# Recurrence: the next pair's key panel inside the state walk, mixing read from the banks, the output in its own buffer beside the new keys, the gate one pair later

## The chip, the cores and the metric

One core of a Trainium2 chip. The metric is the device time of one launch, in microseconds (us). Engines: TensorE (PE; its weight loads are PEld), VectorE (DVE), ScalarE (ACT), GpSimd (POOL), SyncE (SP, which issues the weight DMAs).

## The reference, cut to what matters

Three layers over 512 tokens of width 1024: one with latent and sliding-window attention, one with forgetting attention, and one with an RWKV-7 recurrence beside a convolution. The change touches the recurrence of the third layer alone:

```
rkv = rkv + (shift(rkv) - rkv) * mu_rkv            # shift: the token before
w   = exp(-exp(-softplus(-(w0 + tanh(xw@w1)@w2)) - 0.5));  a = sigmoid(a0 + (xa@a1)@a2)
g   = sigmoid(xg @ g1) @ g2
kk  = k*k_k / max(norm(k*k_k), 1e-12);  k = k*(1 + (a-1)*k_a)
S_t = S_{t-1} diag(w_t) + (S_{t-1} (-kk_t)) (kk_t*a_t)^T + v_t k_t^T ;  o_t = S_t r_t     # per head, 64x64
o   = (o - mean) * rsqrt(var + 64e-5) * ln_g + ln_b            # per head
out = (o + sum(r*k*r_k) * v) * g
```

There are 16 heads of 64 columns.

## The kernel before, in words

Activations lie with features on partitions and the 512 tokens along the free axis. Every product with a weight matrix is done in panels: a panel is 128 output columns, its weights are 128x1024 floats in one of four slots. SP loads the panel into `raw` (L331), ACT casts it to a high part `wh` (`split`, L454), POOL forms the low part `wl` = raw - high (`low`, L1652), and PE multiplies three times per 128 rows (`three`, L1800 to L1802): 24 matmuls of 128x128 by 128x512. Panels are consumed strictly in the order in which `weight_stream` packs them. A slot is cast anew only when PE has counted `panel_done` for the panel that lay in it, and loaded anew when its low part is out.

The recurrence goes over eight pairs of heads (c = 0 to 7; 2 x 64 rows fill the partitions). Pair c takes four panels: a small one with the second factors of decay, rate and gate (`lora_part`), then k, r and v. `pair(c)` on PE issues, in this order: two eighths of the k panel, the mean of the last pair's output (`mean`, L2198), the gate's three matmuls into bank 4, three eighths of k, the variance (`by_token`, L2135), the rest of k, two eighths of r, `output_spread` (L2144, the inverse root spread over rows), more r, the key norm (`kk`, L2135), more r, `kspread` (L2144), the rest of r, all of v, and then `half(c)`. Banks 0 and 1 take turns for the dense tiles; ACT copies each out of its bank (`copy_tile`, L851) into zk, zr, zv, and DVE mixes each with its shifted self in two instructions (`shift`, L1448 and L1449).

`half(n)` is the chunked recurrence: 8 chunks of 64 tokens. Each product is a series of small fp32 matmuls of 64x64 (L2244), in groups g = 0 and 1: l, lr, kr, the bonus (L2193), ab, kv, then the levels that invert a triangular matrix, then tt, mp and n. l needs b (L1473), lr needs r (L1476), kr needs k (L1478). ab needs t1, made from l by DVE (`first_t`, L1527 and L1528, in `half`). The last part is the walk over the states, L2273 to L2286: for each of eight chunks, c (L2277), the output o (L2285, three terms, into the output bank), while DVE adds the next state (L1552). The next pair's decay and rate products are issued early in the levels (`decay_and_rate`).

After the walk ACT copies the output bank into zr (L922); zr holds the output of pair c-1 until DVE has centred it (L1489), scaled it (L1498), added the bonus (L1500) and gated it with the copied gate `gt` (L1502), ACT has taken its high part (L885) and DVE its low part (L1506). Only then may ACT copy the new r into zr. POOL does, within `half`, bd (L1754), kd (L1756), dg (L1757) and the masks of each level (L1765), and the low parts of the panels before and after.

The order on each engine is written out by hand; every engine works its own list in order and waits on counted semaphores.

Of the kernel before, what the change touches and what calls it, by code (L numbers as in the profile page):

```python
# [22 lines left out]
P = 128  # L23
T = 512
# [122 lines left out]
def build(nc, A, n_panels, b2_start):  # L147

    ctx = ExitStack()
    with ctx:  # L150
# [74 lines left out]
        with ExitStack() as part:  # L225


            z = [sb(f"z{n}", [P, T + 1], F32, part) for n in "rkv"]
            zr, zk, zv = (a[:, 1:T + 1] for a in z)
            gt = sb("gt", [P, T], F32, part)  # L230
# [6 lines left out]
            half_b = sb("half_b", [P, 16], F32, part)  # L237
            going = sb("going", [P, T], F32, part)
# [3 lines left out]
        cu, em, rn, kkn = s1, s1c, sd, rs  # L242
        la, lw = t2[:, 0, :], t2[:, 1, :]
# [117 lines left out]
        def groups(names):  # L361
# [4 lines left out]
            pair_act: ["decay", "square", "root", "gate"],  # L366
            pair_dve: ["sums", "mixed", "kmax", "kinverse", "prod"],
# [72 lines left out]
        def _(act):  # L440
# [383 lines left out]
            od0 = NC * 11  # L824

# [5 lines left out]
            def decay_tanh(c):  # L831
                act.wait_ge(mid_done, m0 + 2 * c + 1)
# [3 lines left out]
            def rate_tanh(c):  # L836
                act.wait_ge(mid_done, m0 + 2 * c + 2)
# [8 lines left out]
            def pair(c):  # L846

                def copy_tile(i, dst, p):
                    b = tile_bank(c, i)
                    act.wait_ge(panel_done, p0 + 4 * c + p)  # L850
                    nc.scalar.copy(dst, psum[:, b, :]).then_inc(bank_free[b], 1)  # L851
                if c == 0:
                    split(Idx(0, p0 + 3))
                else:
# [4 lines left out]
                st.did(pair_act, "square", nc.scalar.activation(sq[:, 0, :], zk, ACT.Square, scale=pcol("k_k", c)))  # L859
# [5 lines left out]
                act.wait_ge(panel_done, p0 + 4 * c + 1)  # L865
                st.did(pair_act, "gate", nc.scalar.copy(gt[:, :], psum[:, 4, :]))
                split(Idx(0, p0 + 4 * c + 5))
                act.wait_ge(opnd_dve, c + od0)
                copy_tile(3, zr, 3)
                copy_tile(4, zv, 4)  # L870
                half(c)

            def centred_square(c):

                st.wait(post_dve, c, "centred")
                st.did(post_act, "osquare", nc.scalar.activation(sq[:, 0, :], zr, ACT.Square))
# [5 lines left out]
            def high(c):  # L882

                st.wait(post_dve, c, "out")
                st.did(post_act, "high", nc.scalar.copy(bh[1][:, c, :], zr))  # L885

            def half(n):
# [31 lines left out]
                if not last:  # L919
                    split(Idx(0, p0 + 4 * n + 7))  # L920
                st.wait(half_pe, n, "o7")
                st.did(half_act, "o", nc.scalar.copy(zr, psum[:, O_BANK, :]))  # L922
# [9 lines left out]
            w.p += 4 * NC  # L932
            w.g += 6 * NC
            w.mid += 2 * NC
# [44 lines left out]
        def _(dve):  # L979
# [398 lines left out]
            nc.vector.memset(going[:, :].rearrange("p (a t) -> p a t", t=64)[:, :, 0:1], 0.0)  # L1378
            nc.vector.tensor_scalar(half_b[:, 0:8], par[:, PAR["w0"][0]:PAR["w0"][0] + 8], 0.5, None, ALU.mult)
# [41 lines left out]
            g0 = w.g  # L1421
# [22 lines left out]
            def pair(c):  # L1444

                def shift(i, dst):

                    link(V.tensor_tensor(sq[:, 0, :], z[i][:, 0:T], dst, ALU.subtract))  # L1448
                    return V.scalar_tensor_tensor(dst, sq[:, 0, :], pcol("mu_rkv", NC * i + c), dst, ALU.mult, ALU.add)  # L1449
# [15 lines left out]
                if c:  # L1465
                    output_low(c - 1)
# [17 lines left out]
                V.scalar_tensor_tensor(sq[:, 1, :], psum[:, b, :], 64.0, zv, ALU.mult, ALU.mult).then_inc(bank_free[b], 1)  # L1484
                half(c)

            def centre(c):
                st.wait(post_pe, c, "mean")
                st.did(post_dve, "centred", V.tensor_tensor(zr, zr, psum[:, 2, :], ALU.subtract))  # L1489
# [5 lines left out]
            def output(c):  # L1495

                st.wait(post_pe, c, "ospread")
                link(V.scalar_tensor_tensor(zr, zr, col("lnx_g", c), psum[:, 5, :], ALU.mult, ALU.mult))  # L1498
                tile_moved(c, 5)
                link(V.scalar_tensor_tensor(zr, zr, col("lnx_b", c), sq[:, 1, :], ALU.add, ALU.add))  # L1500
                st.wait(pair_act, c, "gate")
                st.did(post_dve, "out", V.tensor_tensor(zr, zr, gt[:, :], ALU.mult))  # L1502

            def output_low(c):
                st.wait(post_act, c, "high")
                V.tensor_tensor(bl[1][:, c, :], zr, bh[1][:, c, :].bitcast(F32), ALU.subtract).then_inc(opnd_dve, 1)  # L1506

            def half(n):
# [17 lines left out]
                def first_t(g):  # L1526
                    link(V.tensor_tensor(one(g, M_T), bank(f"l.{g}"), each(wm[:, 2, :]), ALU.mult))  # L1527
                    did(f"t1.{g}", V.tensor_tensor(one(g, M_T), one(g, M_T), each(eye[:, :]), ALU.add))  # L1528

# [3 lines left out]
                grouped("l", first_t)  # L1533
# [3 lines left out]
                grouped("ab", first_x)  # L1537
                beside = {8: decay_exponent, 16: decay_sums, 32: rates} if n < NC - 1 else {}
# [25 lines left out]
            output(NC - 1)  # L1564
            output_low(NC - 1)
            w.p += 4 * NC
# [76 lines left out]
        def _(pool):  # L1643
# [124 lines left out]
            def pair(c):  # L1768
# [6 lines left out]
                if c < NC - 1:  # L1775
                    low(Idx(0, p0 + 4 * c + 7))
# [4 lines left out]
            w.p += 4 * NC  # L1781
# [13 lines left out]
        def _(pe):  # L1795
# [327 lines left out]
            def decay_and_rate(c):  # L2123
                p = p0 + 4 * c
                pe.wait_ge(lo_ready, p + 1)
                lora_part(tile_bank(c, 0), p, slice(0, 64), 0, 0).then_inc(mid_done, 1)
                lora_part(tile_bank(c, 1), p, slice(64, 128), 0, 0).then_inc(mid_done, 1)

            def gate(c):
                lora_part(4, p0 + 4 * c, slice(0, 128), P, 1).then_inc(panel_done, 1)  # L2130
# [17 lines left out]
            def pair(c):  # L2148

                def dense_part(b, i, ks):  # L2150

                    p = p0 + 4 * c + i
                    s = p % SLOTS
                    pe.wait_ge(lo_ready, p + 1)
                    for k in ks:
                        if c == 0 and i == 1:
                            pe.wait_ge(opnd_pool, op0 + k + 1)
                        cols = slice(k * P, k * P + P)
                        last = three(psum[:, b, :], wh[:, s, cols], wl[:, s, cols], bh[0][:, k, :], bl[0][:, k, :],
                                     k == 0, k == NC - 1)  # L2160
                    return last
                b = tile_bank(c, 2)
                dense_part(b, 1, range(2))
                if c:
                    mean(c - 1)
                    gate(c)
                    dense_part(b, 1, range(2, 5))
                    variance(c - 1)
                    dense_part(b, 1, range(5, NC)).then_inc(panel_done, 1)
                else:  # L2170
                    dense_part(b, 1, range(2, NC - 1))
                    pe.wait_ge(lora_l, 2)
                    gate(c)
                    dense_part(b, 1, range(NC - 1, NC)).then_inc(panel_done, 1)
                b = tile_bank(c, 3)
                dense_part(b, 2, range(2))
                if c:
                    output_spread(c - 1)
                dense_part(b, 2, range(2, 4))
                st.wait(pair_act, c, "square")  # L2180
                st.did(pair_pe, "kk", by_token(6, sq[:, 0, :]))
                dense_part(b, 2, range(4, 6))
                st.wait(pair_dve, c, "kinverse")
                st.did(pair_pe, "kspread", spread(7, r8[:, 2, :]))
                dense_part(b, 2, range(6, NC)).then_inc(panel_done, 1)
                b = tile_bank(c, 4)
                dense_part(b, 3, range(NC)).then_inc(panel_done, 1)
# [7 lines left out]
            def mean(c):  # L2195
                st.wait(half_act, c, "o")
                st.wait(half_dve, c, "s8")
                st.did(post_pe, "mean", nc.tensor.matmul(psum[:, 2, :], o64[:, :], zr, start=True, stop=True))  # L2198

            def variance(c):  # L2200
                st.wait(post_act, c, "osquare")
                st.did(post_pe, "var", by_token(3, sq[:, 0, :]))
# [5 lines left out]
            def half(n):  # L2208
# [7 lines left out]
                def product(name, *outs, needs=()):  # L2216


                    for g in range(2):
# [3 lines left out]
                        if i == 2:  # L2223
# [257 lines left out]
```

## Time and profile before

| | us |
|---|---|
| median of 3 runs | 2743.78 (2743.17 to 2747.65) |
| profiled execution, its own time | 2744.07 |
| its span | 2742.2 |
| PE busy | 2553.0 (93%) |
| DVE busy | 1395.3 (51%) |
| POOL busy | 1147.4 (42%) |
| ACT busy | 910.6 (33%) |

The recurrence runs from about 1506 us to 2019 us of the span. Pairs repeat every 64.02 us: the copy of the output bank (L922) starts at 1822.29 and again at 1886.31. A row of the timeline gives start, duration, engine, line, operation, output and inputs, and in brackets the idle time before it with what ended it. Ends of matmuls are modelled, so the distance from start to start is what counts on PE.

### The profile page before, as it was taken

To read this page: it belongs to the slowest core of one execution; us is meant where nothing else is said; L and a number is where in the kernel's file an instruction comes from. 1 tells how busy PE (TensorE), PEld (TensorE's weight loads), DVE (VectorE), ACT (ScalarE), POOL (GpSimd) and SP (SyncE) were. 2 spreads that over 40 slices of the span, in tenths; PEclk is the share of its full clock that TensorE was granted. 3 is DMA by queue.
4 is the path that set the end of the run, shared out by engine and by line. 5 is a ranking of instruction groups with operands and counts; after the bars stand their busy time and mean duration, and the time that the engine had idled before them with its cause. 6 is when DMAs were issued, how large, how long until landed. Compare 5 with 4: busy or idle time off the path is not lost.

```text
span 2742.2 us, 46926 instructions
## 1 busy us (share of the span) xinstructions
PE 2553.0 (93%) x18466; PEld 2077.3 (76%) x18466; DVE 1395.3 (51%) x1997; ACT 910.6 (33%) x1444; POOL 1147.4 (42%) x657
## 2 busy tenths in 40 slices
PE   6798899999899998999996999999999988999998
PEld 4575688887787877888875888887887766788886
DVE  3624873345513258454277566666659963321122
ACT  3233422223523334222254333333333334332231
POOL 3433544444444435444454333333333325444442
PEclk8999999999999999999998999999999999999999
DMA  5310223232221112323322111111112222233331
GB/s 152 80 54 16 85 92 100 92 100 85 77 93 35 58 62 85 99 92 94 98 71 73 41 33 41 41 33 33 33 57 87 89 62 83 87 99 98 94 100 54
DMA packets 56465, 202.67 MB, mean 74 GB/s; under 512 B 6768, under 2 KB 7448, under 8 KB 56304
## 3 DMA queue, kind: packets, MB, share of 16 engines
q1 hardware_dynamic: 54144, 195.84, 22.5%
q0 software_dynamic: 1328, 3.68, 0.8%
q8 instruction: 124, 2.03, 0.3%
q10 hardware_dynamic: 832, 0.82, 0.1%
q14 instruction: 37, 0.30, 0.0%
HBM read 196.64 MB, written 3.67 MB: 73 GB/s over the span
## 4 chain that ended last, share of the span: by engine, by line
PE 78%; DVE 11%; issue 4%; ACT 4%; POOL 2%; DMA 0%; DVEq 0%; SPq 0%; ACTq 0%; POOLq 0%
PE banks L1800 21%; PE banks L1801 21%; PE banks L1802 21%; PE banks L2244 8%; ACT sb_pa L635 1%; PE banks L2285 1%; DVE banks L1592 1%; PE banks L2018 1%; DVE sb_zr L1502 1%; POOL sb_pa L1678 1%; PE banks L1980 1%; DVE sb_x L1078 1%; PE banks L2144 1%; PE banks L1933 1%; PE banks L2001 1%
## 5 line engine op out<-in xcount | busy, mean ns | idle before, releaser
L1652 POOL TENSOR_TENSOR sb_wl<-sb_raw,sb_wh 128x1024 fp32r<-128x1024 f32 x365 | 897.3, 2460 | 1235.9 <-ACT sb_wh L454 1235.7
L1800 PE MATMUL banks<-sb_bh,sb_wh 128*128 128x512 f32 x2656 | 1061.8, 400 | 93.9 <-POOL sb_bl L1664 28.0
L1801 PE MATMUL banks<-sb_bl,sb_wh 128*128 128x512 f32 x2656 | 1047.1, 394 | 0.0
L1802 PE MATMUL banks<-sb_bh,sb_wl 128*128 128x512 f32 x2656 | 1045.9, 394 | 0.0
L1800 PEld LDWEIGHTS banks<-sb_bh,sb_wh 128*128 128x128 f32 x2656 | 505.4, 190 | 227.4 <-issue 53.9
L1802 PEld LDWEIGHTS banks<-sb_bh,sb_wl 128*128 128x128 f32 x2656 | 505.1, 190 | 110.5
L1801 PEld LDWEIGHTS banks<-sb_bl,sb_wh 128*128 128x128 f32 x2656 | 505.8, 190 | 107.4 <-issue 2.2
L454 ACT CAST sb_wh<-sb_raw 128x1024 fp32r<-128x1024 f32 x365 | 381.4, 1046 | 542.6 <-PE banks L1802 538.0
L2244 PE MATMUL banks<-sb_m 64*64 64x64 f32 (+1 forms) x5632 | 205.7, 228 | 8.4 <-DVE sb_m L1542 7.6
L2244 PEld LDWEIGHTS banks<-sb_m 64*64 64x64 f32 x5632 | 195.7, 134 | 20.1 <-issue 12.4
L998 DVE SCALAR_TENSOR_TENSOR sb_x<-sb_x,banks 128x512 f32 x72 | 49.5, 688 | 315.0 <-PE banks L1802 315.0
L1057 DVE TENSOR_TENSOR sb_bl<-sb_t,sb_bh 128x512 f32 x64 | 158.9, 2482 | 8.4 <-DVE sb_t L1055 0.7
L1592 DVE SCALAR_TENSOR_TENSOR banks<-sb_ub,sb_cw,banks 128x512 f32<-128x512 f32 x224 | 149.7, 750 | 1.2
L1678 POOL TENSOR_TENSOR sb_pa<-sb_pa,sb_rc 128x256 f32<-128x256 f32 (+3 forms) x128 | 84.1, 681 | 121.7 <-DVE sb_rc L1231 121.7
L473 ACT ACTIVATE sb_sq<-banks 128x512 f32<-128x512 f32 x64 | 38.4, 600 | 238.9 <-PE banks L1802 235.0
L1054 DVE TENSOR_TENSOR sb_bh<-sb_sq 128x512 f32 x64 | 50.1, 783 | 98.8 <-ACT sb_sq L473 98.8
L1765 POOL TENSOR_TENSOR sb_m<-sb_m,sb_wm 128x256 f32<-128x256 f32 x80 | 58.6, 753 | 95.0 <-PE banks L2244 65.2
L635 ACT ACTIVATE sb_pa<-banks,sb_nm 128x256 f32<-128x256 f32 (+3 forms) x128 | 63.8, 503 | 89.7 <-DVE sb_nm L1219 62.3
L1542 DVE TENSOR_TENSOR sb_m<-sb_m,banks 128x256 f32<-128x256 f32 x144 | 59.6, 419 | 53.0 <-PE banks L2244 49.0
L1219 DVE TENSOR_REDUCE sb_nm<-banks 128x1 f32<-128x128 f32 (+3 forms) x96 | 42.2, 481 | 75.3 <-PE banks L1990 75.3
L2001 PE MATMUL banks<-sb_ident,sb_pa 128*128 128x128 f32 x296 | 47.8, 283 | 23.2 <-POOL sb_pa L1678 11.5
L898 ACT COPY sb_m<-banks 128x256 f32<-128x256 f32 x112 | 41.8, 373 | 71.0 <-PE banks L2244 66.0
(319 smaller groups left out, 2628.0 us busy)
## 6 DMA issues: line engine op xcount, KB each, us to landing
sb_raw<-w SPq DMA_DIRECT2D x365, 512.0 KB, 3.5
sb_x<-xT SPq DMA_DIRECT2D x4, 512.0 KB, 6.6
out<-sb_x SPq DMA_DIRECT2D x4, 512.0 KB, 2.7
bias_rows<-sb_brow POOLq DMA_DIRECT2D x1, 1536.0 KB, 35.1
sb_bias<-bias_rows POOLq DMA_DIRECT2D x1, 1024.0 KB, 6.7
sb_pj<-pT POOLq DMA_DIRECT2D x2, 512.0 KB, 3.9
sb_wm<-wm ACTq DMA_DIRECT2D x1, 288.0 KB, 3.4
sb_rope<-rope ACTq DMA_DIRECT2D x1, 256.0 KB, 3.0
```

The source lines that it names most:

```text
L454: nc.scalar.copy(wh[:, s, :], raw[:, s, :]).then_inc(hi_ready, 1)
L635: nc.scalar.activation(pa[:, ring, e, 0:width], psum[:, 4 + 2 * (t % 2) + e, 0:width], ACT.Exp, bias=nm[:, ring, e:e + 1], accum_out=sm[:, ...
L1057: nc.vector.tensor_tensor(bl[hb][:, j.v, :], t2[:, j.k % 2, :], bh[hb][:, j.v, :].bitcast(F32), ALU.subtract).then_inc(opnd_dve, 1)
L1542: grouped(f"{m}{b}", lambda g: did(f"{m}{b}.{g}", V.tensor_tensor(one(g, dst), one(g, dst), bank(f"{m}{b}.{g}"), ALU.add)))
L1592: ins = V.scalar_tensor_tensor(dst, ub[:, tap:tap + T], cw[:, c, tap:tap + 1], acc, ALU.mult, ALU.add)
L1652: nc.gpsimd.tensor_tensor(wl[:, s, :], raw[:, s, :], wh[:, s, :].bitcast(F32), ALU.subtract).then_inc(lo_ready, 1)
L1678: nc.gpsimd.tensor_tensor(p_e, p_e, rc[:, ring, e:e + 1].broadcast_to([P, width]), ALU.mult).then_inc(p_ready, 1)
L1800: nc.tensor.matmul(out, hi_a, hi_b, start=first, stop=False)
L1801: nc.tensor.matmul(out, hi_a, lo_b, start=False, stop=False)
L1802: return nc.tensor.matmul(out, lo_a, hi_b, start=False, stop=last)
L2001: last = nc.tensor.transpose(psum[:, 2 + e, c:c + P], pa[:, t % RING, e, c:c + P], ident[:, :])
L2244: last = nc.tensor.matmul(out, lhs, rhs, start=(t == 0), stop=(t == len(terms) - 1), skip_group_check=True)
```

## The change

Per pair c the panel order becomes k, (decay, rate, gate of pair c-1), r, v, with one more panel at the end for the last gate. The key panel of pair n+1 is multiplied inside the walk of pair n, one eighth (three matmuls) behind each chunk. The v panel moves into `half`, three eighths ahead of l and five behind it. The gate of pair c-1 is multiplied behind `kspread` of pair c, into bank 6, and DVE reads it there; `gt` and its copy go. ACT's copies of k, r and v out of the banks go: DVE mixes from the bank in three instructions (`mix`), one of them a single column. The output has a buffer of its own (`ob`), its squares too (`osq`). DVE's order in a pair is now: mix of k, centre, kmax, kinverse, oinverse, kkn, la, a, b, output_scaled, mix of r, r, k, first_t, output_gated, prod, mix of v, then the masks. PE waits ahead of kr for "out" of the last pair (bank 6).

```diff
@@ VectorE
+                def mix(i, tile, done, own, dst):
+                    b = (g0 + tile) % 2
+                    dve.wait_ge(panel_done, p0 + 4 * c + done)
+                    k = NC * i + c
+                    V.tensor_scalar(dst[:, 0:1], psum[:, b, 0:1], mu_own[:, k:k + 1], None, ALU.mult)
+                    link(V.tensor_scalar(own, psum[:, b, :], mu_own[:, k:k + 1], None, ALU.mult))
+                    V.scalar_tensor_tensor(dst[:, 1:T], psum[:, b, 0:T - 1], pcol("mu_rkv", k), own[:, 1:T], ALU.mult,
+                                           ALU.add).then_inc(bank_free[b], 1)
+                    tile_moved(c, tile)
+                mix(1, 2, 1 if c else 2, kkn, zk)
                 if c:
                     centre(c - 1)
-                    output_inverse(c - 1)
-                tile_moved(c, 2)
-                st.did(pair_dve, "mixed", shift(1, zk))
-                if c:
-                    output(c - 1)
                 st.wait(pair_pe, c, "kk")
...
                 if c:
-                    output_low(c - 1)
+                    output_inverse(c - 1)
                 started(dve, c, half_pe, half_pool)
...
-                tile_moved(c, 3)
-                link(shift(0, zr))
+                if c:
+                    output_scaled(c - 1)
+                mix(0, 3, 3, sq[:, 0, :], zr)
                 st.did(half_dve, "r", ...)
                 link(V.scalar_tensor_tensor(zk, lw, 1.0, zk, ALU.add, ALU.mult))
                 st.did(half_dve, "k", ...)
+                first_t(c)
+                if c:
+                    output_gated(c - 1)
                 st.did(pair_dve, "prod", ...)
-                tile_moved(c, 4)
-                link(shift(2, zv))
-                st.wait(pair_pe, c, "bonus")
-                b = (g0 + 5) % 2
-                V.scalar_tensor_tensor(sq[:, 1, :], psum[:, b, :], 64.0, zv, ...)
+                mix(2, 4, 4, sq[:, 0, :], zv)
                 half(c)
+            def output_gated(c):
+                tile_moved(c, 5)
+                link(V.scalar_tensor_tensor(ob, ob, col("lnx_b", c), sq[:, 1, :], ALU.add, ALU.add))
+                dve.wait_ge(panel_done, p0 + 4 * c + (6 if c < NC - 1 else 5))
+                st.did(post_dve, "out", V.tensor_tensor(ob, ob, psum[:, 6, :], ALU.mult))
@@ in half, behind first_x
+                st.wait(pair_pe, n, "bonus")
+                V.scalar_tensor_tensor(sq[:, 1, :], psum[:, b, :], 64.0, zv, ...)
+                if n:
+                    output_low(n - 1)
@@ ScalarE, pair(c)
-                    centred_square(c - 1)
-                    root_of_output(c - 1)
-                copy_tile(2, zk, 2)
-                st.wait(pair_dve, c, "mixed")
+                act.wait_ge(bank_free[b], c * 3 + (g0 + 2) // 2 + 1)
                 st.did(pair_act, "square", ...)
-                split(Idx(0, p0 + 4 * c + 4))
+                if c:
+                    centred_square(c - 1)
                 st.wait(pair_dve, c, "kmax")
                 st.did(pair_act, "root", ...)
                 if c:
+                    root_of_output(c - 1)
+                split(Idx(0, p0 + 4 * c + 4))
+                split(Idx(0, p0 + 4 * c + 5))
+                if c:
                     high(c - 1)
-                st.did(pair_act, "gate", nc.scalar.copy(gt[:, :], psum[:, 4, :]))
-                split(Idx(0, p0 + 4 * c + 5))
-                copy_tile(3, zr, 3)
-                copy_tile(4, zv, 4)
@@ TensorE, pair(c)
+                if c == 0:
+                    dense_part(0, tile_bank(0, 2), 1, range(NC)).then_inc(panel_done, 1)
+                b = tile_bank(c, 3)
+                dense_part(c, b, 2, range(2))
                 if c:
                     mean(c - 1)
+                dense_part(c, b, 2, range(2, 4))
+                st.wait(pair_act, c, "square")
+                st.did(pair_pe, "kk", by_token(6, sq[:, 0, :]))
+                if c:
                     variance(c - 1)
+                dense_part(c, b, 2, range(4, 6))
+                st.wait(pair_dve, c, "kinverse")
+                st.did(pair_pe, "kspread", spread(7, r8[:, 2, :]))
+                if c:
+                    gate(c - 1)
+                dense_part(c, b, 2, range(6, NC)).then_inc(panel_done, 1)
                 if c:
                     output_spread(c - 1)
                 half(c)
@@ TensorE, half(n)
+                        if name == "kr" and g == 0 and n:
+                            st.wait(post_dve, n - 1, "out")
...
+                v_bank = tile_bank(n, 4)
+                dense_part(n, v_bank, 3, range(3))
                 product("l", ...)
+                dense_part(n, v_bank, 3, range(3, NC)).then_inc(panel_done, 1)
                 product("lr", ...)
                 product("kr", ...)
                 bonus(n)
...
                     st.did(half_pe, f"o{ch}", last)
+                    if n < NC - 1:
+                        last = dense_part(n + 1, k_bank, 0, range(ch, ch + 1))
+                        if ch == 7:
+                            last.then_inc(panel_done, 1)
@@ weight_stream
+        cols, before = slice(c * P, c * P + P), slice(max(c - 1, 0) * P, max(c, 1) * P)
+        lora = filled(np.concatenate([second[:, cols], I["gate_g2_2"][0][:, before]], axis=1))
+        out += [k[c], lora, r[c], v[c]] if c else [lora, k[c], r[c], v[c]]
+    out.append(filled(I["gate_g2_2"][0][:, -P:]))
```

## Rows read from the trace of the kernel before

**Rows 1.** The page: busy time, share of the span and instructions of each engine.
```profile
PE 2553.0 (93%) x18466; PEld 2077.3 (76%) x18466; DVE 1395.3 (51%) x1997; ACT 910.6 (33%) x1444; POOL 1147.4 (42%) x657
```

**Rows 2.** Busy time in one pair (window, us, PE, PEld, DVE, ACT, POOL, clock, DMA, GB/s).
```profile
1822.20:1886.20 64.00, 59.90 (x1095) 52.11 (x1094) 40.15 (x67) 22.49 (x40) 21.14 (x17) 1.00 0.11 35
```

**Rows 3.** What PE waited for in one pair, 1822.20 to 1886.22 (total, times, longest).
```profile
PE banks L2244 <- DVE sb_m L1528: 1.7, 1, 1.7
...
PE banks L2244 <- DVE sb_m L1542: 0.7, 1, 0.7
```

**Rows 4.** PE's timeline of that pair: walk, dense, spread, l to kr, ab.
```profile
1821.41 0.33 PE L2277 MATMUL banks<-sb_m_s,sb_m 64*64 64x64 f32 x4
...
1822.18 0.50 PE L1800 MATMUL banks<-sb_bh,sb_wh 128*128 128x512 f32 x1
1822.52 0.39 PE L1801 MATMUL banks<-sb_bl,sb_wh 128*128 128x512 f32 x1
...
1837.89 1.09 PE L2144 MATMUL banks<-sb_ident,sb_r 128*64 128x128 f32 x16 [1.18 <-DVE sb_r L1464]
1838.91 0.50 PE L1800 MATMUL banks<-sb_bh,sb_wh 128*128 128x512 f32 x1
...
1845.63 0.39 PE L1802 MATMUL banks<-sb_bh,sb_wl 128*128 128x512 f32 x1
1845.95 4.64 PE L2244 MATMUL banks<-sb_m 64*64 64x64 f32 x96
1850.53 1.13 PE L2193 MATMUL banks<-sb_sq,sb_mask 128*128 128x512 f32 x2
1853.31 2.25 PE L2244 MATMUL banks<-sb_eye,sb_m 64*64 64x64 f32 x68 [1.65 <-DVE sb_m L1528]
...
1880.54 0.33 PE L2277 MATMUL banks<-sb_m_s,sb_m 64*64 64x64 f32 x4
```

**Rows 5.** DVE's timeline in the same pair.
```profile
1824.80 0.69 DVE L1489 TENSOR_TENSOR sb_zr<-sb_zr,banks 128x512 f32<-128x512 f32 x1 [2.79 <-PE banks L2198]
...
1834.45 2.83 DVE L1502 TENSOR_TENSOR sb_zr<-sb_zr,sb_gt 128x512 f32<-128x512 f32 x1
...
1839.13 0.75 DVE L1469 SCALAR_TENSOR_TENSOR sb_w<-sb_zk,sb_par,banks 128x512 f32<-128x512 f32 x1 [0.30 <-PE banks L2144]
1839.91 2.66 DVE L1470 TENSOR_TENSOR sb_t<-sb_w,sb_t 128x512 f32<-128x512 f32 x1
...
1848.60 1.55 DVE L1448 TENSOR_TENSOR sb_sq<-sb_zv 128x512 f32<-128x512 f32 x1
1850.18 1.43 DVE L1449 SCALAR_TENSOR_TENSOR sb_zv<-sb_sq,sb_par,sb_zv 128x512 f32<-128x512 f32 x1
...
1852.82 0.43 DVE L1528 TENSOR_TENSOR sb_m<-sb_m,sb_eye 128x256 f32<-128x256 f32 x1
...
1853.96 2.47 DVE L1523 TENSOR_TENSOR sb_m<-banks,sb_wm 128x512 f32<-128x512 f32 x4
```

**Rows 6.** POOL's timeline in the same pair.
```profile
1834.35 2.38 POOL L1652 TENSOR_TENSOR sb_wl<-sb_raw,sb_wh 128x1024 fp32r<-128x1024 f32 x1 [13.84 <-ACT sb_wh L454]
1839.62 2.40 POOL L1652 TENSOR_TENSOR sb_wl<-sb_raw,sb_wh 128x1024 fp32r<-128x1024 f32 x1 [2.88 <-ACT sb_wh L454]
...
1848.10 1.50 POOL L1756 TENSOR_TENSOR sb_m<-sb_m,sb_ep 128x512 f32<-128x512 f32 x1 [2.68 <-DVE sb_m L1478]
1849.56 1.50 POOL L1757 TENSOR_TENSOR sb_m<-sb_eye,sb_ep 128x512 f32<-128x512 f32 x1
1854.72 1.42 POOL L1765 TENSOR_TENSOR sb_m<-sb_m,sb_wm 128x256 f32<-128x256 f32 x2 [3.66 <-DVE sb_m L1523]
```

**Rows 7.** The chain in the same pair: mean and variance on PE.
```profile
1823.84 0.86 PE banks L2198 x2
1827.45 0.79 PE banks L2135 x8
```

**Rows 8.** ACT's timeline in the same pair: the table ahead of the root.
```profile
1826.18 1.28 ACT L880 ACT_TABLE_LOAD   x1
```

More of the change, by code:

```diff
@@ L365, in build @@
             pair_pe: ["kk", "kspread", "bonus"],
-            pair_act: ["decay", "square", "root", "gate"],
-            pair_dve: ["sums", "mixed", "kmax", "kinverse", "prod"],
+            pair_act: ["decay", "square", "root"],
+            pair_dve: ["sums", "kmax", "kinverse", "prod"],
             post_pe: ["mean", "var", "ospread"],
@@ L918, in half @@
                 move("n", M_N)
-                if not last:
-                    split(Idx(0, p0 + 4 * n + 7))
+                split(Idx(0, p0 + 4 * n + 7))
                 st.wait(half_pe, n, "o7")
-                st.did(half_act, "o", nc.scalar.copy(zr, psum[:, O_BANK, :]))
+                st.did(half_act, "o", nc.scalar.copy(ob, psum[:, O_BANK, :]))
             decay_tanh(0)
@@ L1493, in output_inverse, with output_scaled, first_t @@
                 st.did(post_dve, "oinverse", V.reciprocal(r8[:, 4, :], r8[:, 3, :]))
-            def output(c):
+            def output_scaled(c):
                 st.wait(post_pe, c, "ospread")
-                link(V.scalar_tensor_tensor(zr, zr, col("lnx_g", c), psum[:, 5, :], ALU.mult, ALU.mult))
+                link(V.scalar_tensor_tensor(ob, ob, col("lnx_g", c), psum[:, 5, :], ALU.mult, ALU.mult))
+            def output_gated(c):
                 tile_moved(c, 5)
-                link(V.scalar_tensor_tensor(zr, zr, col("lnx_b", c), sq[:, 1, :], ALU.add, ALU.add))
-                st.wait(pair_act, c, "gate")
-                st.did(post_dve, "out", V.tensor_tensor(zr, zr, gt[:, :], ALU.mult))
+                link(V.scalar_tensor_tensor(ob, ob, col("lnx_b", c), sq[:, 1, :], ALU.add, ALU.add))
+                dve.wait_ge(panel_done, p0 + 4 * c + (6 if c < NC - 1 else 5))
+                st.did(post_dve, "out", V.tensor_tensor(ob, ob, psum[:, 6, :], ALU.mult))
             def output_low(c):
                 st.wait(post_act, c, "high")
-                V.tensor_tensor(bl[1][:, c, :], zr, bh[1][:, c, :].bitcast(F32), ALU.subtract).then_inc(opnd_dve, 1)
+                V.tensor_tensor(bl[1][:, c, :], ob, bh[1][:, c, :].bitcast(F32), ALU.subtract).then_inc(opnd_dve, 1)
+            def first_t(n):
+                for g in range(2):
+                    st.wait(half_pe, n, f"l.{g}")
+                    link(V.tensor_tensor(one(g, M_T), bank(f"l.{g}"), each(wm[:, 2, :]), ALU.mult))
+                    st.did(half_dve, f"t1.{g}", V.tensor_tensor(one(g, M_T), one(g, M_T), each(eye[:, :]), ALU.add))
             def half(n):
@@ L1563, in _ @@
             output_inverse(NC - 1)
-            output(NC - 1)
+            output_scaled(NC - 1)
+            output_gated(NC - 1)
             output_low(NC - 1)
-            w.p += 4 * NC
+            w.p += 4 * NC + 1
             w.g += 6 * NC
@@ L1780, in _ @@
                 pair(c)
[L1781 removed]
+            w.p += 4 * NC + 1
             panels(4 * NC)
@@ L2148, in pair @@
             def pair(c):
[L2150 to L2161, printed above, removed]
@@ L2177, in pair @@
+                st.wait(pair_dve, c, "kinverse")
+                st.did(pair_pe, "kspread", spread(7, r8[:, 2, :]))
+                if c:
+                    gate(c - 1)
+                dense_part(c, b, 2, range(6, NC)).then_inc(panel_done, 1)
                 if c:
                     output_spread(c - 1)
[L2179 to L2187, printed above, removed]
                 half(c)
@@ L2197, in mean @@
                 st.wait(half_dve, c, "s8")
-                st.did(post_pe, "mean", nc.tensor.matmul(psum[:, 2, :], o64[:, :], zr, start=True, stop=True))
+                st.did(post_pe, "mean", nc.tensor.matmul(psum[:, 2, :], o64[:, :], ob, start=True, stop=True))
             def variance(c):
                 st.wait(post_act, c, "osquare")
-                st.did(post_pe, "var", by_token(3, sq[:, 0, :]))
+                st.did(post_pe, "var", by_token(3, osq[:, :]))
             def output_spread(c):
```

95 lines of the change are left out of this document (45 added, 50 removed).

## The prediction

> **What bounds the kernel now.** I read the page first: PE is busy 93% of the span [rows 1], so a gain must come from time in which PE waits, and anything added to PE's list costs its full length. The busy time by stage says the same of the recurrence: in a pair of 64.0 us PE is busy 59.9, DVE 40.2, POOL 21.1, at full granted clock [rows 2]. Then I asked what PE waits for in one pair: 1.65 us ahead of ab, for t1 from DVE, 1.18 ahead of `kspread`, for the inverse key norm, 0.7 in the levels and, in the timeline, 0.3 in the walk, whose 5.66 us are that much more than eight chunks of 0.66 and the step to dense work (both below) [rows 3, 4]. The first two and the last, 3.1 us in a pair, are what this change can reach; the 0.7 is in a part that it leaves alone. Last I read DVE beside POOL, because both long waits come from DVE. An instruction with both inputs in SBUF that is issued while POOL works ends 0.55 us after POOL's: gating takes 2.83 (POOL's low part runs from 1834.35 to 1836.73), la takes 2.66 (1839.62 to 1842.02), the two mixing instructions of v take 1.55 and 1.43 (kd to 1849.60, dg to 1851.06) [rows 5, 6]. With one input in a bank it isn't held: the four masks take 2.47 together, 0.62 each, beside POOL's mask [rows 5, 6]. These held instructions are the reason of the 1.18 (kmax stands behind the gating) and of most of the 1.65.
>
> **The walk.** Before, a pair's walk lasts from 1880.54 to the first dense matmul at 1822.18 + 64.02 = 1886.20, 5.66 us, and its chunks follow at 0.66 (c at 1821.41, the next would have been at 1822.07). After, three dense matmuls stand behind each chunk. From c to the second dense matmul the trace shows 1822.52 - 1821.41 = 1.11; one more spacing of 0.23 brings the third (24 + 6 matmuls between 1838.91 and 1845.95 are 0.23 each); from the last dense matmul to the first small one is 0.32 (1845.63 to 1845.95) [rows 4]. That makes 1.66 a chunk; eight, less 0.09 for the last, which is followed by dense work, are 13.2, and I take 13.1 since a chunk need not wait for DVE any more (0.04 to hide in 0.66, and the 0.3 behind chunk 0 is hidden too). The k panel's own 24 matmuls are 5.5 of this. So 7.6 stands where 5.66 was: changing seven more times between small and dense work costs about 0.3 each, more than the 0.3 wait that it fills. Bounds: the price of a change could be 0.1 (only the way back, 0.32 against 0.23), which makes the walk 11.7, or 0.4, 13.9.
>
> **From the walk to kspread.** Counted from T, the end of the walk's last dense matmul. PE: two eighths of r 1.4, mean 0.87, two eighths 1.4, kk 0.9, variance 0.8, two eighths 1.4: kspread at T + 6.8 [rows 4, 7]. Does anything come late? k is mixed at T + 1.8 (a column, estimated 0.1, one instruction from the bank and one with the bank shifted: 0.69 and 0.75 by the nearest rows [rows 5]; neither bound, 0.43 as for half the columns or 0.75, moves PE), its square is out at T + 2.6, wanted at 3.6. Mean, centring (0.69) and the output's squares are out at 3.9, wanted at 4.5. kmax comes at 4.7; ACT's root stands behind a table load of 1.28 [rows 8] that starts at 3.9, so the root is out at 5.5 and the inverse at 5.7, wanted at 6.8. The 1.18 goes, and what is late next has 1 us of cover. ACT's three copies out of the banks and the copy of the gate cost nothing before or after except the one of k (0.6, on the chain just walked). The output buffer frees the new r from waiting for the old output's low part; what that is worth is in the places that DVE's steps take below.
>
> **From kspread to ab.** Let X be the start of kspread. PE: spread 1.0, gate and two eighths of r 2.2, output_spread 1.1, three eighths of v 2.3: l at X + 6.55. DVE: kkn starts at X + 1.24 (1839.13 against 1837.89) and la at X + 2.0. POOL's low part of the next key panel runs from X + 0.1 to 2.5 (ACT casts it behind the roots), so la ends at 3.0, a at 3.7. ACT casts the following panel only when the gate has released its slot, at X + 2.0 to 3.1; its low part holds POOL from 3.1 to 5.5, and b, issued at 3.7, ends at 6.1. l isn't late, by 0.5. PE goes on: l 1.0, five eighths of v with two changes 3.7, lr 1.8: ready for kr at X + 13.0 (l, lr and kr are 1845.95 to 1850.53, 4.6 for 32 matmuls each; l writes half as wide, so I divide 1.0, 1.8, 1.8). kr waits for "out", and DVE's list behind b is: output_scaled 0.78, mix of r 1.6, r 0.6, new k 0.7, k 0.6, which is out at X + 10.4. There POOL starts kd and dg, 1.5 each, until X + 13.4. first_t is four instructions of 0.43; two read only SBUF. By the rule of the rows the first ends behind kd (12.3), the second behind dg (13.7). Then the bonus 0.78 and the gate from its bank 0.69: out at X + 15.2. PE waits 2.2 us. kr 1.8, bonus 1.0, and ab starts at X + 18.0. Queued behind that wait are all of kr, bonus, ab and the levels; nothing else of PE's can pass.
>
> No row shows an instruction of 256 columns held by POOL. If these aren't held, out comes at X + 13.4 and the wait is 0.4; if they are, 2.2; if the low part at 3.1 also catches "a" (issued 0.04 before it), l waits 0.2 and the wait grows to 2.9. I take 2.2: the held rows are of four kinds, and they have both inputs in SBUF in common, not their size. The Trainium skill bears on just this (GPSIMD Engine Reference, Key points): GpSimd shares its SBUF interfaces with VectorE, and contends with instructions that have two SBUF inputs or run in a two-port mode. By it size plays no part and the wait is 2.2; by the rows alone 0.4 stays possible. The trace agrees as far as it goes, with the 2.66 of la.
>
> **The sum for a pair**, from the walk's first chunk to the next ab: before 5.66 + (1853.31 - 1822.18) = 36.8. After 13.1 + 6.8 + 18.0 = 37.9. That is +1.1 us. Checked as a difference: -3.1 of waits, +2.2 of a new one, seven changes +2.0, the change around l +0.25, kk and variance side by side -0.2, which is +1.15. Behind ab nothing moves: DVE reaches the end of first_x at ab + 3.6, the second output step and the low part make it 4.9, and t2's result isn't wanted before ab + 7. It happens seven times: +7.7. In pair 0 the gate's three matmuls leave (-0.7), and a low part that isn't held back by a gate comes sooner and holds both a and b, so l waits (PE at X + 4.6, b at 6.9) and ab comes as late as X + 16.2 against 15.4 (+0.8): +0.1. Behind the last pair the last gate is added: three matmuls, +0.7 at most. The extra panel's DMA, cast (1.05) and low part (2.4) lie under PE's work: POOL is idle 43 of 64 us [rows 2]; the added column of constants on DVE is under 0.2. In all +8 against the profiled execution's own 2744.1, which stands 0.3 above the median: 2751.8 against a median of 2743.8.
>
> **Rivals.**
> 1. *DVE reaches out in time* (faster). Place: the list between b and out. It decides when out comes before X + 13.0, that is 2.2 sooner than I count; being free of kd and dg gives 1.8 of it, being free of the low part at b another 1.8 (b at 4.3). For it: no held row has 256 columns, and the instructions read from a bank are free. Against: every 512-wide one with two SBUF inputs that met POOL was held. Then a pair is 1.1 faster than before, -7 in all: 2736.5; with changes at the lower price, 11.7 for the walk, -2.5 a pair: 2727.
> 2. *Only first_t is free*, b is held: wait 0.4, a pair 0.7 faster: -4.5, 2739.5. No change that can be told.
> 3. *"a" is held too*, or changes cost 0.4: +0.7 to +0.9 a pair more: 2757.
> 4. *The panel in the walk costs only its matmuls* while DVE is late as I say: walk 11.7, a pair -0.3: 2742.
>
> **Chances.** My forecast 0.5 (2748 to 2755), rival 1 0.17, rival 2 0.12, rival 3 0.11, rival 4 0.1. The range 2734 to 2758 leaves out the fast end of rival 1 and the far end of rival 3, about 2 in 10. A measurement of this kernel tells a change from none at about 0.2%, 5.5 us: slower is above 2749.3, that is most of my forecast and rival 3, 0.52; faster is below 2738.3, rival 1 and some of rival 2, 0.22; the rest 0.26.
>
> **What the profile would show.** Right: chunks of the walk 1.6 to 1.7 apart; no wait ahead of kspread and of ab; one ahead of kr, near 2.2, ended by the gated output (ob); first_t's second instruction lasting over a microsecond beside kd and dg; b lasting over 2; pairs 65.1 apart. Wrong: chunks below 1.5 apart, or no wait ahead of kr: then pairs are under 64.02. A second wait ahead of l, or of kk, would mean that a chain is longer than I count.

## The result, and the profile after

The changed kernel takes 2751.8 us (median of 11 runs, 2748.0 to 2755.8) against 2744.1 of the kernel before (11 runs, 2742.7 to 2747.7). The ratio is 1.0027, 95% interval 1.0019 to 1.0034: slower by about 7 us. The profiled executions have spans of 2750.8 and 2742.2.

First PE's waits in one pair of the changed kernel (what waited, for what, total, times, longest), 1822.1 to 1886.5:

```profile
PE banks L2250 <- DVE sb_w L1503: 1.6, 1, 1.6
PE banks L2250 <- DVE sb_m L1549: 1.2, 1, 1.2
```

The 1.7 ahead of ab [rows 3] and the 1.18 ahead of kspread [rows 4] are gone. A new wait, 1.6 ahead of kr, stands in their place (L1503 gates the old output). The one in the levels is as it was: [rows 3] have 0.7 there, but in a pair that is longer than the others, and the other five middle pairs of the kernel before have 1.2. What the long pair, 1822.2 to 1886.2, has in exchange:

```profile
PE banks L2244 <- issue: 0.5, 2, 0.3
```

Then the busy times, of the same stretch as above in the changed kernel and of an ordinary pair of the kernel before (columns as in [rows 2]):

```profile
1758.91:1822.20 63.29, 59.14 (x1095) 51.87 (x1094) 40.14 (x67) 22.48 (x40) 21.14 (x17) 1.00 0.11 35
1822.10:1886.50 64.40, 61.63 (x1098) 51.59 (x1095) 37.62 (x70) 20.43 (x36) 20.15 (x17) 1.00 0.11 35
```

PE is busy 2.5 us more than in an ordinary pair before (1.7 more than in that of [rows 2]), with the same matmuls, and waits 1.4 less. Where the busy time grew, the timeline shows (chunks of the walk, then kspread, l, lr, kr, bonus, ab):

```profile
1821.88 0.33 PE L2288 MATMUL banks<-sb_m_s,sb_m 64*64 64x64 f32 x4
...
1822.61 0.50 PE L1807 MATMUL banks<-sb_bh,sb_wh 128*128 128x512 f32 x1
1822.95 0.40 PE L1808 MATMUL banks<-sb_bl,sb_wh 128*128 128x512 f32 x1
...
1823.51 0.33 PE L2288 MATMUL banks<-sb_m_s,sb_m 64*64 64x64 f32 x4
...
1825.18 0.33 PE L2288 MATMUL banks<-sb_m_s,sb_m 64*64 64x64 f32 x4
...
1835.11 0.40 PE L1807 MATMUL banks<-sb_bh,sb_wh 128*128 128x512 f32 x1
...
1841.99 1.09 PE L2169 MATMUL banks<-sb_ident,sb_r 128*64 128x128 f32 x16
...
1848.56 1.15 PE L2250 MATMUL banks<-sb_m 64*64 64x64 f32 x32
...
1853.27 1.96 PE L2250 MATMUL banks<-sb_m 64*64 64x128 f32 x32
1856.81 1.96 PE L2250 MATMUL banks<-sb_m 64*64 64x128 f32 x32 [1.58 <-DVE sb_w L1503]
1858.70 1.12 PE L2199 MATMUL banks<-sb_sq,sb_mask 128*128 128x512 f32 x2
1859.76 2.25 PE L2250 MATMUL banks<-sb_eye,sb_m 64*64 64x64 f32 x68
```

In the kernel before, the chunk ahead of the last one started so:

```profile
1820.75 0.33 PE L2277 MATMUL banks<-sb_m_s,sb_m 64*64 64x64 f32 x4
```

Chunks now follow at 1.67 (1823.51 to 1825.18). Before they followed at 0.66 (1820.75 to the 1821.41 of [rows 4]), and three dense matmuls alone are 0.69: that leaves 0.32 for each change to dense work and back. The walk with its panel takes 13.2 us (to 1835.11), where walk and panel apart were 11.2. Now DVE and POOL from kspread (1841.99) on:

```profile
1845.47 2.88 DVE L1471 TENSOR_TENSOR sb_m<-sb_t,sb_w 128x512 f32<-128x512 f32 x1
...
1852.06 0.69 DVE L1477 TENSOR_TENSOR sb_m<-sb_zk,sb_w 128x512 f32<-128x512 f32 x1
1852.67 0.42 DVE L1512 TENSOR_TENSOR sb_m<-banks,sb_wm 128x256 f32<-128x256 f32 x1
1853.12 1.05 DVE L1513 TENSOR_TENSOR sb_m<-sb_m,sb_eye 128x256 f32<-128x256 f32 x1
1854.10 0.41 DVE L1512 TENSOR_TENSOR sb_m<-banks,sb_wm 128x256 f32<-128x256 f32 x1
1854.54 0.83 DVE L1513 TENSOR_TENSOR sb_m<-sb_m,sb_eye 128x256 f32<-128x256 f32 x1
1855.30 0.74 DVE L1501 SCALAR_TENSOR_TENSOR sb_w<-sb_w,sb_par,sb_sq 128x512 f32<-128x512 f32 x1
1856.07 0.69 DVE L1503 TENSOR_TENSOR sb_w<-sb_w,banks 128x512 f32<-128x512 f32 x1
```

```profile
1841.90 2.38 POOL L1660 TENSOR_TENSOR sb_wl<-sb_raw,sb_wh 128x1024 fp32r<-128x1024 f32 x1 [16.01 <-ACT sb_wh L456]
1845.20 2.59 POOL L1660 TENSOR_TENSOR sb_wl<-sb_raw,sb_wh 128x1024 fp32r<-128x1024 f32 x1 [0.93 <-ACT sb_wh L456]
1848.51 1.06 POOL L1762 TENSOR_TENSOR sb_m<-sb_m,sb_ep 128x512 f32<-128x512 f32 x1 [0.72 <-DVE sb_m L1471]
1852.84 1.06 POOL L1764 TENSOR_TENSOR sb_m<-sb_m,sb_ep 128x512 f32<-128x512 f32 x1 [3.27 <-DVE sb_m L1477]
1853.85 1.24 POOL L1765 TENSOR_TENSOR sb_m<-sb_eye,sb_ep 128x512 f32<-128x512 f32 x1
```

b (L1471) is held by the second low part, which ends at 1847.79; b ends 0.56 later. The second instruction of first_t (L1513), 0.43 in [rows 5], takes 1.05 beside kd (to 1853.90) and 0.83 beside dg (to 1855.09), and ends 0.27 and 0.28 after them. So an instruction of 256 columns is held too. (An instruction is called held when it lasts longer for GpSimd's work beside it and ends only behind it.)

**The account.** From the first matmul of pair 0 to the first of the next stage the kernel before takes 1506.43 to 2018.81 = 512.4, the changed one 1508.27 to 2026.73 = 518.5: +6.1. Of it pair 0 up to its walk gives -0.85 (56.73 to 55.88), the seven distances from walk to walk +6.6 (442.24 to 448.81, 0.94 each on average) and the end +0.36. The other 2.5 of the spans lie in stages that the change doesn't touch: 1.8 ahead, 0.7 behind. In all the profiles here that first matmul starts between 1504.9 and 1509.4, with the same code ahead of it, and the part behind the recurrence takes 720.7 to 724.7, so these 2.5 say nothing of the change.

### The profile page after: what moved, and what is told of

It is laid out like the page before. It is cut to its first block, busy times and chain, and to the rows that moved or that the text cites. A ratio compares the mean times of both kernels' runs of the same rounds, so it can differ in the third digit from the quotient of the medians.

```text
span 2750.8 us, 46944 instructions
## 1 busy us (share of the span) xinstructions
PE 2572.4 (94%) x18466; PEld 2075.8 (75%) x18466; DVE 1379.4 (50%) x2022; ACT 894.9 (33%) x1413; POOL 1140.5 (41%) x658
## 4 chain that ended last, share of the span: by engine, by line
PE 76%; DVE 13%; issue 5%; ACT 4%; POOL 2%; DMA 0%; DVEq 0%; SPq 0%; ACTq 0%; POOLq 0%
PE banks L1807 21%; PE banks L1808 20%; PE banks L1809 20%; PE banks L2250 7%; PE banks L2296 1%; ACT sb_pa L637 1%; DVE banks L1600 1%; PE banks L2025 1%; POOL sb_pa L1686 1%; PE banks L1987 1%; DVE sb_x L1072 1%; PE banks L1940 1%; PE banks L2008 1%; DVE sb_w L1432 1%; PE banks L2288 1%
## 5 line engine op out<-in xcount | busy, mean ns | idle before, releaser
L893 ACT COPY sb_m<-banks 128x256 f32<-128x256 f32 x112 | 41.7, 372 | 69.9 <-PE banks L2250 64.8
```

## The experiments

The theory: the change gives back two waits and pays for it in two places that lie one behind the other on PE's list, the changes between small and dense work in the walk, and a late gated output, held up by POOL. (Small work is the matmuls of 64x64, dense work those of the panels.) Below, a pitch is the time from one copy of the output bank to the next (ACT L916, L922 in the kernel before), in the middle pairs of the profile: 64.4 for the changed kernel, for the one before 63.3 to 63.5 in five pairs and 64.0 in one, which was the pair of [rows 2 to 7]. Medians are of 4 to 10 runs; those of the kernel before on the same chips were 2744.5 to 2744.9.

### The old output gated early

```diff
                 if c:
                     output_scaled(c - 1)
+                    output_gated(c - 1)
                 mix(0, 3, 3, sq[:, 0, :], zr)
...
                 first_t(c)
-                if c:
-                    output_gated(c - 1)
```

> The changed kernel, with the old output gated on VectorE right behind its scaling, ahead of the mix of r, so that out is ready long before PE wants kr. My theory: the 1.6 us that PE waits ahead of kr come from two of first_t's instructions held by GpSimd's kd and dg, and from VectorE's order. Then the wait ahead of kr goes; the new k comes 1.4 later, which is still in time; prod comes later, and about 0.5 of wait appears ahead of the bonus. A pair takes 63.2 instead of 64.4, the whole about 2743 against 2751.8. Rival (the wait ahead of kr is only where lateness of all of VectorE's list shows): the same 1.6 reappear ahead of the bonus or ab, a pair stays at 64.2 to 64.4, the whole at 2751.

Measured: 2746.3 (ratio to before 1.0004, 0.9995 to 1.0014), pitch 63.5. PE's waits in a pair:

```profile
PE banks L2249 <- DVE sb_m L1548: 1.2, 1, 1.2
PE banks L2198 <- DVE sb_sq L1480: 0.9, 1, 0.9
```

The wait ahead of kr is gone; 0.9 of it, not 0.5, came back ahead of the bonus. So the pair is 0.85 shorter, not 1.2: the theory holds, and the rival has half a point, since DVE's list was late by more than the one item.

### The key panel behind the walk

```diff
-                if c == 0:
-                    dense_part(0, tile_bank(0, 2), 1, range(NC)).then_inc(panel_done, 1)
+                dense_part(c, tile_bank(c, 2), 0 if c else 1, range(NC)).then_inc(panel_done, 1)
...
                     st.did(half_pe, f"o{ch}", last)
-                    if n < NC - 1:
-                        last = dense_part(n + 1, k_bank, 0, range(ch, ch + 1))
-                        if ch == 7:
-                            last.then_inc(panel_done, 1)
```

> The changed kernel, with the next pair's key panel taken out of the walk and multiplied in one piece behind it, ahead of the r panel; all else as in the change. My theory: each of the seven additional changes between small and dense work costs 0.28 on PE, and the walk has only 0.3 of wait to fill, so a pair is 1.7 to 1.8 shorter, 62.6, and the whole about 2739.5. Rival (the walk is bound by the answer of VectorE, so that dense work in it is nearly free): taking it out lets the walk fall back to its latency, 5.7, and the pair stays at 64.4 or grows; the whole 2751 or more.

Measured: 2734.0 (0.9964, 0.9950 to 0.9978), pitch 62.4. One pair, by the copies of the output bank:

```profile
1755.63 0.59 ACT L916 COPY sb_w<-banks 128x512 f32<-128x512 f32 x1 [4.20 <-PE banks L2293]
1818.02 0.59 ACT L916 COPY sb_w<-banks 128x512 f32<-128x512 f32 x1 [4.20 <-PE banks L2293]
```

2.0 less in a pair, a little more than expected. Seven times that are 14; the median fell by 17.8, and in this profile 3.3 of the difference in span lie behind the recurrence (720.7 against 724.1), which this edit doesn't touch. Without its part in the walk the change is faster than the kernel before. PE waits for the same two as in the changed kernel, 1.6 and 1.2.

### The key panel in the walk, in two pieces

```diff
-                    if n < NC - 1:
-                        last = dense_part(n + 1, k_bank, 0, range(ch, ch + 1))
+                    if n < NC - 1 and ch in (0, 7):
+                        last = dense_part(n + 1, k_bank, 0, range(4) if ch == 0 else range(4, NC))
```

> The changed kernel, with the key panel in the walk in two pieces of four eighths, behind chunks 0 and 7, instead of one eighth behind each of the eight chunks. My theory (each change between small and dense work costs a fixed 0.3 on PE; one piece behind the walk took a pair from 64.4 to 62.4): six changes fewer, and the piece behind chunk 0 still fills the wait of 0.3, so a pair takes 62.4 and the whole is about 2735. Rival (what costs is that dense work lies in the walk at all, whatever the number of pieces): 64.0 and 2749.

Measured: 2737.1 (0.9970, 0.9960 to 0.9980), pitch 62.4, the waits as in the changed kernel. It is the number of changes that costs: six fewer give 2.0, 0.33 each. The piece behind chunk 0 pays for its one change with the 0.3 wait that it fills. The median stands 3 above that of the panel behind the walk at the same pitch, and the two profiles differ by 3.5 behind the recurrence: that is scatter.

### Both, then prod first

> Both of the edits before: the output gated early, and the key panel behind the walk. My theory: the two costs lie one behind the other on PE's list, so they add: a pair takes 61.4, the whole about 2731, faster than the kernel before (2744). Rival (they share a bound, VectorE's list): the sum is no better than the better one alone, 2739 to 2743.

Measured: 2731.9 (0.9956, 0.9939 to 0.9972), pitch 61.55. The pitches add: -2.0 and -0.85 are 61.55. The medians don't add as well (17.8 and 5.5 against 19.9), which is their scatter. The pitch also closes from the other side: an ordinary pair before, 63.3, less its two waits of 1.65 and 1.18, plus the 0.9 ahead of the bonus and 0.33 for the change around l, is 61.7, 0.15 above what was measured.

```diff
-                first_t(c)
                 st.did(pair_dve, "prod", ...)
+                first_t(c)
```

> Gate early, key panel behind the walk, and prod ahead of first_t on VectorE. In the kernel with the first two edits PE waits 0.9 ahead of the bonus, for prod. My theory: prod then comes 1.8 earlier, ahead of the end of kr, and t1 is still in time for ab, one bonus (1.0) later: the wait goes, a pair takes 60.7 instead of 61.55, the whole about 2726. Rival (VectorE's list as a whole is late, the wait only moves): 0.5 or more appear ahead of ab, for t1, and the pair is at 61.2 or above.

Measured: 2727.6 (0.9934, 0.9918 to 0.9951), pitch 61.2. The wait ahead of the bonus is gone and ab starts 0.95 sooner after kspread, as expected; yet the pitch fell by 0.3 only, to what the rival had said. But not in the rival's way: no wait is listed ahead of ab. From kspread to the levels' matmuls behind the next pair's products it is 23.3 against 23.6, so 0.6 of the 0.95 is lost between ab and there. Those products, decay and rate (64 rows each), show where the 0.6 went. First the kernel of the run before this one, then this one, on DVE and on PE:

```profile
1786.64 0.50 PE L1806 MATMUL banks<-sb_lha,sb_wh 64*128 64x512 f32 x2
```

```profile
1787.65 0.68 DVE L1541 SCALAR_TENSOR_TENSOR sb_sq<-banks,sb_zv 128x512 f32<-128x512 f32 x1
```

```profile
1787.81 0.50 PE L1806 MATMUL banks<-sb_lha,sb_wh 64*128 64x512 f32 x1
1788.15 0.39 PE L1807 MATMUL banks<-sb_lla,sb_wh 64*128 64x512 f32 x1
1788.38 0.50 PE L1806 MATMUL banks<-sb_lha,sb_wh 64*128 64x512 f32 x1
1788.38 0.39 PE L1808 MATMUL banks<-sb_lha,sb_wl 64*128 64x512 f32 x1
1788.72 0.39 PE L1807 MATMUL banks<-sb_lla,sb_wh 64*128 64x512 f32 x1
1788.95 0.39 PE L1808 MATMUL banks<-sb_lha,sb_wl 64*128 64x512 f32 x1
```

The rate's bank is freed by that DVE instruction at 1788.33, and its three matmuls start only then. Before, each ran beside one of the decay's three ("x2" above), in the other half of the rows. No wait shows, since PE is never empty. This was a new theory at that point; the last run below tests it.

### dg ahead of kd on POOL

```diff
-            half_pool: ["bd", "kd", "dg"] ...
+            half_pool: ["bd", "dg", "kd"] ...
```

(and the two instructions exchanged)

> The changed kernel, with GpSimd's dg issued ahead of kd, so that it runs while VectorE reads from a bank, and no longer while first_t's last instruction wants SBUF. My theory of the holds: that instruction takes 0.42 instead of 0.83, the wait ahead of kr falls from 1.6 to 1.2, a pair to 64.0, the whole to about 2749. Rival (first_t's 1.05 and 0.83 have another cause than kd and dg): no change, 2751.8.

Measured: 2748.6 (1.0016, 1.0006 to 1.0026), pitch 64.0 in three of the six middle pairs and 64.2 to 64.6 in the others, and the wait ahead of kr is 1.2. DVE's first_t in it:

```profile
1848.68 1.05 DVE L1513 TENSOR_TENSOR sb_m<-sb_m,sb_eye 128x256 f32<-128x256 f32 x1
1849.66 0.41 DVE L1512 TENSOR_TENSOR sb_m<-banks,sb_wm 128x256 f32<-128x256 f32 x1
1850.10 0.42 DVE L1513 TENSOR_TENSOR sb_m<-sb_m,sb_eye 128x256 f32<-128x256 f32 x1
```

The first is still held, by kd; the second, 0.83 in the changed kernel, takes 0.42 with POOL elsewhere, and all 0.4 arrive at PE's wait. The holds are POOL's doing, and the rival (another cause than kd and dg) is out.

### v in one piece ahead of l

```diff
-                dense_part(n, v_bank, 3, range(3))
+                dense_part(n, v_bank, 3, range(NC)).then_inc(panel_done, 1)
                 product("l", ...)
-                dense_part(n, v_bank, 3, range(3, NC)).then_inc(panel_done, 1)
```

> The changed kernel, with the v panel in one piece ahead of l instead of three eighths ahead and five behind. My theory: PE has one change between dense and small work less (0.3), but l comes 3.4 later and with it first_t on VectorE, which was the late chain at kr; out comes about 0.3 later than now, the wait ahead of kr grows from 1.6 to 2.1 to 2.3, and a pair takes 64.5 to 64.8. Rival (out doesn't depend on l's place): a pair takes 64.1.

Measured: 2750.8 (1.0024, 1.0014 to 1.0033), pitch 64.4, the wait ahead of kr 1.9 to 2.0. The change around l is saved and comes back as wait: kr starts 14.8 behind kspread as in the changed kernel, since it is bound by out. But out didn't come later, as I had expected: l was done when DVE reached first_t (10.70 behind kspread, 10.68 in the changed kernel). So the rival's premise, that out doesn't depend on l's place, is right, and its price is wrong: with out where it was, PE's saving had to become wait. My numbers (2.1 to 2.3, 64.5 to 64.8) were near for a reason that was half wrong. One pair of this profile took 66.0, at a granted clock of 0.97 where its neighbours had 1.00.

### The low part behind the scan

```diff
-                split(Idx(0, p0 + 4 * n + 6))
                 move("z32", M_Z)
+                split(Idx(0, p0 + 4 * n + 6))
```

> The kernel of the run before this one, with ScalarE's cast of the panel next but one (r) behind the moves of the last level instead of ahead of them, so that GpSimd's low part starts after VectorE's scan. My theory: the scan (two SBUF inputs, 2.4 instead of 1.23 beside the low part) is held like the others, and is what PE waits 1.1 for in the last level; then it takes 1.23 and that wait falls to 0.3 or less: a pair takes 59.8, the whole about 2720. Rival (the wait in the last level is set by the level's own steps, and the scan lies beside it): the wait stays at 1.1 and the time at that of the run before.

Measured: 2723.0 (0.9914, 0.9897 to 0.9931), pitch 60.2. The wait of 1.2 in the levels, which the kernel before had too, is gone altogether: the rival is out. Of the 1.2 a pair keeps 1.0 (61.2 to 60.2); the theory had 59.8. The scan in the changed kernel, then DVE and POOL of this one:

```profile
1813.59 2.40 DVE L1432 TENSOR_TENSOR_SCAN sb_w<-sb_going,sb_t 128x512 f32<-128x512 f32 x1
```

```profile
1797.75 1.22 DVE L1432 TENSOR_TENSOR_SCAN sb_w<-sb_going,sb_t 128x512 f32<-128x512 f32 x1
...
1799.84 2.54 DVE L1436 TENSOR_SCALAR sb_t<-sb_t 128x512 f32<-128x512 f32 x1
```

```profile
1799.74 2.35 POOL L1659 TENSOR_TENSOR sb_wl<-sb_raw,sb_wh 128x1024 fp32r<-128x1024 f32 x1 [3.33 <-ACT sb_wh L456]
```

The scan takes 1.22, not 2.40. The low part now holds another instruction, L1436, with one SBUF input only (0.41 in the changed kernel, 2.54 here), and nothing waits for that one.

### The best version

```diff
                 masked("kr", M_AK, M_RK)
+                st.wait(pair_pe, n, "bonus")
...
+                V.scalar_tensor_tensor(sq[:, 1, :], psum[:, b, :], 64.0, zv, ...)
                 st.wait(half_dve, n, "kr.1")
                 grouped("ab", first_x)
-                st.wait(pair_pe, n, "bonus")
...
-                V.scalar_tensor_tensor(sq[:, 1, :], psum[:, b, :], 64.0, zv, ...)
```

(with dg ahead of kd, on top of the kernel just shown)

> The kernel of the run with the late low part, with two more moves: VectorE scales the bonus out of its bank ahead of first_x instead of behind it, and GpSimd does dg ahead of kd. In the run with prod ahead of first_t a pair reached ab 0.95 earlier, but lost 0.6 again right behind: the bank of the next pair's rate was freed at 1788.33, so its three matmuls no longer ran beside those of the decay. My theory: freed 1.7 earlier, they run in pairs again, and a pair takes 59.6 instead of 60.2; the whole is about 2718. Rival (the two sets of three run one behind the other for another reason, such as their order): a pair stays at 60.2, the whole at 2723.

Measured: 2714.7 (0.9890, 0.9870 to 0.9909), pitch 59.6. DVE is done with the bonus at 1778.72, before PE wants the bank, and the decay and rate products run in pairs again:

```profile
1778.04 0.68 DVE L1539 SCALAR_TENSOR_TENSOR sb_sq<-banks,sb_zv 128x512 f32<-128x512 f32 x1
```

```profile
1780.67 0.50 PE L1806 MATMUL banks<-sb_lha,sb_wh 64*128 64x512 f32 x2
1781.01 0.40 PE L1807 MATMUL banks<-sb_lla,sb_wh 64*128 64x512 f32 x2
1781.23 0.40 PE L1808 MATMUL banks<-sb_lha,sb_wl 64*128 64x512 f32 x2
```

Two edits were made at once here; the profiles tell them apart. From kspread to ab it is 16.0 in this kernel and in the one with the late low part, so dg ahead of kd gives PE nothing up to there. It saves DVE 0.4 (first_t's second instruction is at 0.42 again), but the bonus leaves its bank 1.9 before PE wants it, so this isn't needed either, as far as can be worked out without a run of its own. From kspread to the levels' matmuls behind the products it is 22.7 against 23.3, and that is the whole 0.6. This version beats the kernel before by 30 us and the changed one by 37.

## Why the prediction was right

- **The sum for a pair.** 37.9 was predicted from the walk's first chunk to the next ab; the changed kernel takes 1859.76 - 1821.88 = 37.9.
- **The walk.** Chunks at 1.66, measured 1.67; 13.1, measured 13.2. The key panel put behind the walk again gives back 2.0 a pair, which is the term: seven changes of 0.33 less the 0.3 of wait.
- **From the walk to kspread.** T + 6.8, measured 6.9 (1835.11 to 1841.99), with nothing late. ACT's table load and the inverse had the cover that was counted.
- **From kspread on.** l at X + 6.6 (predicted 6.55), lr at 11.3 (11.2), out at 14.8 (15.2), ab at 17.8 (18.0). The wait ahead of kr is 1.6, not 2.2, and three terms make that up. kd and dg took 1.06 and 1.24, where I had set 1.5 each from [rows 6]: 0.7 too much. The new k was there at 10.8, not 10.4, most of it because the low part under b took 2.59 and b ended at 6.4, not 6.1. And PE was ready for kr at 13.2, not 13.0. So the errors partly cancel.
- **The open choice.** Whether 256 columns are held had no row. The Trainium skill (GPSIMD Engine Reference, Key points) names two SBUF inputs as the condition and no size, and I followed it. The trace agrees: L1513 at 1.05 and 0.83, and at 0.42 once dg had moved.
- **Pair 0.** Predicted +0.1, measured -0.85. I had kspread 0.7 sooner for the gate's three matmuls; it starts 1.36 sooner (13.46 behind the first matmul against 14.82), and 0.3 of the rest is the wait ahead of kk, which goes. From there ab comes at 15.9, where I had 16.2 and the kernel before has 15.4. l does wait for b, 1.8, because the second low part holds a, which takes 2.76.
- **The pitch.** "Pairs 65.1 apart" was wrong, they are 64.4. I had read the pitch of the kernel before off its one long pair, 64.02; the others are at 63.3 to 63.5. The sum didn't use the pitch, only 36.8 of walk to ab, and this is the same in the long pair and in the one before it: the 0.7 lie behind ab. From walk to walk the difference is 1.0 to 1.2 in five of the seven, 0.4 in the long one and 0.85 in the last: 6.6 instead of 7.7. Why one pair was long, no run here shows.
- **The exact number is luck.** The code's own effect is 6.1 in the profile, and 8 was predicted; the terms as written, 7.7, 0.1 and at most 0.7, even add up to 8.5. That the median came out at the very 2751.8 owes 1.6 to scatter, well inside the interval (5 to 9 us). The sign and the mechanism don't rest on it.

The rivals: that DVE reaches out in time (rival 1) is refuted by the 1.6 wait and by the holds it needed not to be, b at 2.88 and L1513; that only first_t is free (2) is refuted by L1513; that "a" is held too (3) happens in pair 0 and in no other (a takes 2.76 there and 0.69 in all seven others), since it is issued 0.3 before the second low part in a middle pair; that the panel costs only its matmuls (4) is refuted by the panel in two pieces and behind the walk.

## What to carry to other kernels

Small matmuls and dense panels should be kept in long pieces on PE. Filling a wait with a dense piece pays only if the wait is longer than the change there and back, which was 0.33 here; this change paid it seven more times for one wait of 0.3. When a wait is moved off one engine's list, walk the whole list of the engine that releases it, with GpSimd's instructions beside it: an instruction that reads SBUF twice there, and some that read it once (L1436), lasts until GpSimd is done and a little longer. And a list of waits shows only when PE is empty: two matmul streams that stopped running side by side cost 0.6 a pair and showed as busy time. Last, read a period off several repeats, not off one.

## What the runs showed of the hardware

- VectorE and GpSimd hold each other, both ways. VectorE's instruction with two SBUF inputs ends 0.56 after GpSimd's where it has 512 columns and 0.27 after it where it has 256; the scan of 512 columns ends 1.07 after it. That is each time its free duration (0.69, 0.42, 1.22) less 0.13 to 0.15.
- GpSimd's kd takes 1.06 when VectorE reads a bank beside it. It takes 1.50 where VectorE is in the middle of an SBUF instruction as it starts [rows 6], and again 1.50 once prod had been put ahead of first_t:

```profile
1778.37 0.74 DVE L1479 SCALAR_TENSOR_TENSOR sb_sq<-sb_zr,sb_par,sb_zk 128x512 f32<-128x512 f32 x1
```

```profile
1778.53 1.50 POOL L1763 TENSOR_TENSOR sb_m<-sb_m,sb_ep 128x512 f32<-128x512 f32 x1 [4.98 <-DVE sb_m L1478]
```

  The low part takes 2.38 and 2.59 in the same way. So a duration taken from a crowded row is too long for an empty place.
- It isn't only instructions with two inputs: a tensor_scalar from SBUF to SBUF (L1436) took 2.54 beside a low part, 0.41 without. The Trainium skill (GPSIMD Engine Reference, Key points) says that VectorE's instructions in a two-port mode contend with GpSimd as well. This trace agrees, if L1436 runs in such a mode, which no run shows by itself. The tensor_scalar from a bank, L1448, took 0.74 and wasn't held, though GpSimd's bd ran beside it (1848.51 to 1849.57).
- A 128x512 tensor_scalar costs 0.41 from SBUF (L1436) and 0.74 from a bank (L1448), and one of a single column costs 0.22, of which 0.14 is seen as distance to the next (1835.38 to 1835.52).
- A change between 64x64 matmuls and dense ones and back costs PE 0.32 to 0.33. The runs show the price, not its reason.
